# One stream of the expert table for tiles 2 to 4 in place of three tiles of gathers

## The reference

```python
eidx = jnp.take_along_axis(cidx, pos, axis=-1)          # cidx = i1 * 128 + i2
gate = jax.nn.softmax(top, axis=-1)
act = jax.nn.gelu(jnp.einsum('thkd,td->thk', u[eidx], xc), approximate=False)
return jnp.einsum('thk,thkd->td', gate * act, v[eidx])  # u, v: 16384 rows of 1024 floats
```

## Time and profile before

| what | value |
|---|---|
| runs | 4024.05, 4027.4, 4028.98 us |
| the profiled execution | span 4023.9 us; it has no other time of its own, and the runs lie 0.1 to 5.1 us above it |
| first dot product | at 920.8 us |
| last dot product | at 3953.9 us |
| moved by DMA | 1422.97 MB, 1086.75 of it by POOL's queue q0 (the gathers) |
| busy | PE 69%, DVE 61%, POOL 53%, ACT 21% |

### The profile page before, as it was taken

The page is one execution under the profiler, slowest core; times in us unless marked ns, Lnnn a source line. Parts: engine busy times, 40 slices in busy tenths (PEclk is TensorE's granted clock), DMA queues, the critical chain, the costliest instruction groups (busy, mean ns, idle before and its releaser), DMA issues.

```text
span 4023.9 us, 41489 instructions
## 1 busy us (share of the span) xinstructions
PE 2788.8 (69%) x14155; PEld 1429.4 (36%) x14155; DVE 2439.3 (61%) x5186; ACT 858.2 (21%) x2057; POOL 2121.6 (53%) x2149
## 2 busy tenths in 40 slices
PE   6899999898975677796676767455757753333334
PEld 4787777544342322333333323122323320000000
DVE  4552446527676666556766665677766667666652
ACT  4333213402143301112333011132320110000000
POOL 1000205013576656556766565676665667777775
PEclk9999999999987888897887888778888875565566
DMA  8944865567999999999999999999999999999998
GB/s 223 258 154 143 228 209 169 180 240 268 413 407 393 403 410 412 413 412 393 393 400 405 412 400 413 401 406 397 392 406 411 389 409 409 410 408 408 402 409 336
DMA packets 472416, 1422.97 MB, mean 354 GB/s; under 512 B 66152, under 2 KB 136784, under 8 KB 464016
## 3 DMA queue, kind: packets, MB, share of 16 engines
q0 software_dynamic: 298768, 1086.75, 69.5%
q1 hardware_dynamic: 173152, 332.95, 23.2%
q10 hardware_dynamic: 288, 0.62, 0.1%
HBM read 1359.46 MB, written 90.06 MB: 360 GB/s over the span
## 4 chain that ended last, share of the span: by engine, by line
DMA 38%; POOL 13%; PE 9%; issue 8%; DVE 8%; ACT 0%; SPq 0%; DVEq 0%; ACTq 0%; POOLq 0%
DMA ring<-in_peer_u,idx 34%; POOL ring L2459 6%; POOL ring L2452 6%; PE ps_l L1775 5%; DMA ring<-in_peer_v,idxT 4%; DVE ring L2637 4%; PE acc L2683 2%; PE ps_l L1853 1%; PE ps_l L1831 0%; DMA lane<-state_scr 0%; DVE e_f L2560 0%; PE ps_l L1848 0%; DVE hit L2558 0%; DVE where L2520 0%; DVE rest L2521 0%
## 5 line engine op out<-in xcount | busy, mean ns | idle before, releaser
L2637 DVE CUSTOM_DVE_ANT_0 ring<-ring,ps_n2F 128x1024 f32<-128x1024 f32 x1024 | 1242.2, 1220 | 933.3 <-DMA ring<-in_peer_u,idx 922.2
L2459 POOL DMA_INDIRECT ring<-in_peer_u,idx x1024 | 999.1, 976 | 805.8 <-DVE dots L2637 576.3
L2683 PE MATMUL acc<-ring,spread 128*32 128x512 f32 x4096 | 734.7, 853 | 953.3 <-DMA ring<-in_peer_v,idxT 953.1
L2452 POOL DMA_INDIRECT ring<-in_peer_v,idxT x1024 | 993.0, 970 | 336.5 <-issue 297.5
L1775 PE MATMUL ps_l<-lane 128*128 128x512 f32 x1760 | 790.2, 603 | 11.6 <-ACT lane L2100 6.6
L2683 PEld LDWEIGHTS acc<-ring,spread 128*32 128x32 f32 x4096 | 147.7, 136 | 1417.6 <-issue 1415.7
L1775 PEld LDWEIGHTS ps_l<-lane 128*128 128x128 f32 x1760 | 330.8, 193 | 443.8 <-issue 431.4
L562 POOL DMA_DIRECT2D bias<-rpb_scr x16 | 13.2, 829 | 322.5 <-PE ps_dt L846 277.0
L1970 PE MATMUL ps_l<-lane 128*128 128x512 f32 x192 | 117.3, 696 | 56.1 <-DVE nmax L2152 55.8
L2489 ACT ACTIVATE dots<-dots 128x32 f32<-128x32 f32 x32 | 7.3, 229 | 606.1 <-DVE dots L2637 605.9
L2060 ACT ACTIVATE st<-st,nmax 128x512 f32<-128x512 f32 x128 | 92.2, 720 | 184.0 <-DVE nmax L2152 182.9
(11 more groups left out here) (363 smaller groups left out, 4014.7 us busy)
## 6 DMA issues: line engine op xcount, KB each, us to landing
lane<-kept_scr SPq DMA_DIRECT2D x44, 2048.0 KB, 10.6
w_z<-in_w_in SPq DMA_DIRECT2D x16, 1024.0 KB, 6.0
adaB<-in_w_ada SPq DMA_DIRECT2D x16, 1024.0 KB, 6.2
ring<-in_peer_u,idx POOLq DMA_INDIRECT x1024
ring<-in_peer_v,idxT POOLq DMA_INDIRECT x1024, 13.8
kept_scr<-in_w_in SPq DMA_DIRECT2D x6, 2048.0 KB
lane<-w_scr SPq DMA_DIRECT2D x6, 2048.0 KB, 10.9
ada<-in_w_ada SPq DMA_DIRECT2D x8, 1024.0 KB, 15.4
```

Source lines behind the costliest of these rows:

```text
L2452: pool.indirect_dma_start(v_rows[:, nv % RV, :], None, a["peer_v"][0], bass.IndirectOffsetOnAxis(ap=idxT[:, m % 2, col:col + 1], axis=0)). ...
L2459: pool.indirect_dma_start(u_rows[:, n % RU, :], None, a["peer_u"][0], bass.IndirectOffsetOnAxis(ap=idx[:, i % RI, j:j + 1], axis=0)).then_ ...
L2637: nc.vector.tensor_tensor_reduce(out=u_rows[:, n % RU, :], in0=u_rows[:, n % RU, :], in1=ps_n[:, :], scale=1.0, scalar=0.0, op0=ALU.mult, ...
L2683: last = nc.tensor.matmul(acc[q * QUAD:(q + 1) * QUAD, cols], spread[:, m % 2, c0:c0 + QUAD], v_rows[:, nv % RV, cols], start=(g == 0 and ...
```

## The change

V of tiles 2, 3 and 4 is no longer gathered. Their picks and weights are kept (`idx_f` and `weight` get RH = 4 rows) until the tile's 128 picks are weighted, then:

1. PE transposes the tile's picks and weights (`turn_picks`), and DVE splits the expert's number into its two keys (`split_picks`).
2. For each token ACT makes a one-hot matrix of the first key (two instructions: the square of the difference, and relu(1 - 2 x), 128 picks x 128 keys), DVE one of the second key times the weight (`second_hot`), and PE multiplies them (`make_parts`): the token's weight for each of the 128 x 128 experts. Four tokens go together; ACT evicts them to a buffer for 16 tokens, and then stores the buffer (1 MB, in pieces of 512 bytes) in the main memory. This goes on in the slots of the tile after, a batch of four tokens every three slots.
3. From slot 770 to 1046 SP loads the table V once, 32 blocks of 2 MB (four first keys each), and the stored weights, 16 x 3 loads of 512 KB; PE multiplies each block (192 units of four matmuls 128x128 by 512, `multiply_block`) and DVE adds each unit's result to a sum in SBUF (`add_block`). The buffers are those of the lane.
4. At the end DVE norms the three tiles together (`whole_sum` and what follows).

V of the other tiles is gathered as before; that of tiles 0 and 1 is spread over the slots of tiles 0 to 4 (a gather every 2.5 slots), that of tiles 5 to 7 keeps its slots. The ring of V is 10 rows, of which 7 are used until slot 768; the residual of a tile has a row of its own.

```diff
-    RU, RV, RI = 6, 12, 2
+    RU, RV, RI, RH = 6, 10, 2, 4
...
+        parts = v_rows[:, RV - 2:RV, :].rearrange("p r d -> p (r d)")
...
-        TURN_I_AT, IDXT_AT = 14, 20
-        FETCH_AT, SUM_AT = 13, 16
+        TURN_I_AT, IDXT_AT, TURN_W_AT, SPREAD_AT = -26, -25, -9, -8
+        FETCH_AT = 45
+        PICK_TURN_AT, SPLIT_AT, PART_AT, PART_STEP = 4, 5, 9, 3
...
+        pace = GRAINS * (DENSE[-1] + 1) / (GRAINS * len(BEFORE))
+
+        def fetch_slot(s, k):
+
+            m = v_grain[s]
+            if m < GRAINS * DENSE[0]:
+                return FETCH_AT + int(pace * (s * GRAIN + k))
+            return m * GRAIN + FETCH_AT + k
+
+        ALL_ROWS_FROM = PICKS * len(BEFORE) + 84
+        v_row = [nv % (RV - 3) if nv < ALL_ROWS_FROM else (nv - ALL_ROWS_FROM) % RV for nv in range(len(SUMMED) * PICKS)]
...
+            n += PART_AT - PICK_TURN_AT
+            for k in range(P // TURNS):
+                while turning & {n, n + 1}:
+                    n += 1
+                part_mm_at[n], part_ev_at[n + 1] = i * P // TURNS + k, i * P // TURNS + k
+                for r, before in enumerate((2, 2, 1, 1)):
+                    hot_at.setdefault(n - before, []).append(i * P + k * TURNS + r)
+                n += PART_STEP
...
+        DENSE_FROM, DENSE_TO, DENSE_LAG = PICKS * 6 + 2, PICKS * TT + 22, 2
+        unit_slot = [DENSE_FROM + q * (DENSE_TO - DENSE_FROM) // ALL_BLOCK_UNITS for q in range(ALL_BLOCK_UNITS)]
...
+        def load_shares(sp, c):
...
+            if c >= 2:
+                sp.wait_ge(block_mm, (c - 1) * UNITS_A_SHARE)
+            sp.dma_start(v_block[:, c % 2, :, :], v_blocks[c]).then_inc(s_block[c % 2], 16)
+            s, first = divmod(c * KEYS_TOGETHER, PART_KEYS)
+            if first == 0:
+                if s == 0:
+                    sp.wait_ge(s_stored, 16 * ND * P // PART_TOKENS)
+                for i in range(ND):
+                    sp.dma_start(shares[s % 2][i], share_scr[i][s].rearrange("b g n -> b (g n)")).then_inc(s_part[s % 2], 16)
...
                 (ScalarE, in its slot)
+                        for u in hot_at.get(n, ()):
+                            act.wait_ge(picks_split, u // P + 1)
+                            if u >= TURNS:
+                                act.wait_ge(part_mm, u - TURNS + 1)
+                            if u:
+                                act.wait_ge(hot_a_done, u)
+                            nc.scalar.activation(off_key, every_key[:, :], ACT.Square, bias=pickT[:, 0, u % P:u % P + 1], scale=1.0).then_inc(squared, 1)
+                            act.wait_ge(squared, u + 1)
+                            nc.scalar.activation(hot_a[:, u % TURNS, :], off_key, ACT.Relu, bias=1.0, scale=-2.0).then_inc(hot_a_done, 1)
+                        if n in part_ev_at:
+                            k = part_ev_at[n]
+                            group, turn = divmod(k * TURNS, PART_TOKENS)
+                            act.wait_ge(part_mm, (k + 1) * TURNS)
+                            if k and turn == 0:
+                                act.wait_ge(s_stored, 16 * group)
+                            nc.scalar.activation(parts.rearrange("p (c t e) -> p t c e", t=PART_TOKENS, e=PART_KEYS)[:, turn:turn + TURNS, :, :],
+                                                 ps_turn[:, :].rearrange("p (t c e) -> p t c e", t=TURNS, e=PART_KEYS), ACT.Copy).then_inc(part_ev, 1)
+                            if turn == PART_TOKENS - TURNS:
+                                act.wait_ge(part_ev, k + 1)
+                                d, g = divmod(group, P // PART_TOKENS)
+                                nc.scalar.dma_start(share_scr[d][:, :, g, :].rearrange("c b n -> b c n"),
+                                                    parts.rearrange("p (c n) -> p c n", n=PART_KEYS * PART_TOKENS)).then_inc(s_stored, 16)
...
                 (VectorE)
+                def second_hot(u):
+
+                    if u >= TURNS:
+                        v.wait_ge(part_mm, u - TURNS + 1)
+                    k = u % P
+                    nc.vector.tensor_scalar(hot_b[:, u % TURNS, :], every_key[:, :], pickT[:, 1, k:k + 1], pickT[:, 2, k:k + 1], ALU.is_equal, ALU.mult).then_inc(hot_b_done, 1)
+
+                def add_block(q):
...
+                    v.wait_ge(block_mm, q + 1)
+                    if c == 0:
+                        nc.vector.tensor_copy(total, bank).then_inc(block_added, 1)
+                    else:
+                        v.wait_ge(block_added, q - UNITS_A_SHARE + 1)
+                        nc.vector.tensor_tensor(total, total, bank, ALU.add).then_inc(block_added, 1)
...
                 (TensorE)
+                def make_parts(k):
+
+                    pe.wait_ge(hot_a_done, (k + 1) * TURNS)
+                    pe.wait_ge(hot_b_done, (k + 1) * TURNS)
+                    turned_bank_read("parts", k)
+                    for r in range(TURNS):
+                        nc.tensor.matmul(ps_turn[:, r * P:(r + 1) * P], hot_b[:, r, :], hot_a[:, r, :], start=True, stop=True).then_inc(part_mm, 1)
+
+                def multiply_block(q):
...
+                    if q % UNITS_A_SHARE == 0:
+                        pe.wait_ge(s_block[c % 2], 16 * (c // 2 + 1))
+                        s = c * KEYS_TOGETHER // PART_KEYS
+                        pe.wait_ge(s_part[s % 2], 16 * ND * (s // 2 + 1))
+                    if q >= LANE_BANKS:
+                        pe.wait_ge(block_added, q - LANE_BANKS + 1)
+                    s, first = divmod(c * KEYS_TOGETHER, PART_KEYS)
+                    share = shares[s % 2][i].rearrange("p (n e) -> p e n", e=PART_KEYS)
+                    for k in range(KEYS_TOGETHER):
+                        last = nc.tensor.matmul(bank, share[:, first + k, :], v_block[:, c % 2, k, half * HALF:(half + 1) * HALF],
+                                                start=(k == 0), stop=(k == KEYS_TOGETHER - 1))
+                    last.then_inc(block_mm, 1)
```

More of the change, by code:

```diff
@@ L2387, in normed_row @@
             return tok[:, [k for k, kind in enumerate(tok_kind) if kind == ("n2", t)][0] % RT, :]
+        SUMMED = [t for t in range(TT) if t not in DENSE]
+        BEFORE = [t for t in SUMMED if t < DENSE[0]]
+        order = {t: i for i, t in enumerate(SUMMED)}
+        v_grain = [GRAINS * t + g for t in SUMMED for g in range(GRAINS)]
+        pace = GRAINS * (DENSE[-1] + 1) / (GRAINS * len(BEFORE))
[4 more added lines that the diff above has]
+            return m * GRAIN + FETCH_AT + k
@@ new lines, in stage_tail @@
+        for c in range(SHARES):
+            block_at.setdefault(unit_slot[(c - 1) * UNITS_A_SHARE] + 1 if c >= 2 else DENSE_FROM - 6 + c, []).append(c)
+        WHOLE_SUM = DENSE_TO + DENSE_LAG + 2
+        RESIDUAL_SLOT, WHOLE_ROOT, WHOLE_NORM = PICKS * (TT - 1) + 8, WHOLE_SUM + 3 * ND + 1, WHOLE_SUM + 3 * ND + 4
+        LANE_JOBS = len(evac_of)
+        LANE_ACTS, LANE_DVES = acts, dves
+        DROOM = KEYS_TOGETHER * DM
+        v_block = lane[:, 0:2 * DROOM].rearrange("p (r a d) -> p r a d", r=2, a=KEYS_TOGETHER)
@@ new lines, in stage_tail @@
+        share_rooms = [lane[:, 2 * DROOM + r * DM:2 * DROOM + (r + 1) * DM] for r in range(2 * ND - 1)] + [gin[:, 0:2, :].rearrange("p r n -> p (r n)")]
+        shares = [[share_rooms[r * ND + i] for i in range(ND)] for r in range(2)]
+        whole = [st_room[:, 0:DM], st_room[:, DM:2 * DM], qcol[:, :, :, :].rearrange("p r k n -> p (r k n)")]
+        residual = [tok[:, 0, :], tok[:, 1, :], n2[:, :]]
+        v_blocks = a["peer_v"][0].rearrange("(c i b) d -> c b i d", i=KEYS_TOGETHER, b=NKEYS)
@@ L2440, in _ @@
                         n = i * PICKS + j
-                        m, k = fetched(n)
-                        if m is not None:
+                        for m, k in fetch_at.get(n, ()):
                             nv = m * GRAIN + k
@@ L2566, in experts @@
                         v.wait_ge(u_used, (t - RI) * PICKS + (g + 1) * GRAIN)
[L2567 removed]
+                    nc.vector.tensor_copy(idx[:, t % RI, picks], idx_f[:, t % RH, picks]).then_inc(topk_done, 1)
                     if t >= 2:
@@ L2645, in _, with turned_bank_read @@
             def _(pe):
+                turned_last = [None]
+                def turned_bank_read(kind, number):
+                    if turned_last[0] is not None:
+                        was, i = turned_last[0]
+                        if was == "index":
+                            pe.wait_ge(idxT_done, i + 1)
+                        elif was == "weight":
+                            pe.wait_ge(spread_done, TOGETHER * (i + 1))
+                        elif was == "picks":
+                            pe.wait_ge(picks_split, i + 1)
+                        else:
+                            pe.wait_ge(part_ev, i + 1)
+                    turned_last[0] = kind, number
                 def turn(src, c0, done):
```

311 lines of the change are left out of this document (221 added, 90 removed).

## The result

The changed kernel takes 4200.4 us, the median of 4 runs (4199.2 to 4207.5), beside 4028.1 of the kernel before: ratio 1.0438 (95% interval 1.0423 to 1.0453), slower by 172 us. The forecast was slower by 24 (4051), with 4180 as its upper end. The profiled execution spans 4197.5 us.

What follows compares the result with a forecast made beforehand. DMA time was taken as the bound; by stretch, -199 (tiles 0 to 2), -44 (3 to 5) and +267 (6, 7 and the end) made +24 on 4023.9 us, so 4051 us, range 3905 to 4180.

Steps and rivals of the forecast that it cites:

- Tiles 0 to 2: First stretch, 1184.3 us before: DMA floor 915 plus 70 us gives 985, a gain of 199 us (bounds 269 and 124).
- 92% and 97% at once were never shown: First three tiles: doubt that DVE (848 us) and PE (885 us) could stay so busy near the 915 us DMA floor.
- rival 1: All tiles: DMA stays full throughout; 174 us less, 3853 us, or 3950 with half the margins; chance 0.31.
- I take 3 us a time: 63: Tiles 3 to 5: DVE's stand when ACT waits for a store's landing, 0 to 11 us possible, 21 times.
- 43 for the tie: Tiles 3 to 5: cost of ACT, DVE and PE waiting on each other through four reused one-hot buffers, 43 us.
- the floor of 1034: Tiles 3 to 5: DMA time from 1184.2 us, 235 less for fewer V gathers, 85 more for the stores.
- The stretch's own worst case: Tiles 3 to 5: loss of 116 us, at 21 x 11 = 231 for store waits and 35 more for the tie.
- rival 2: Tiles 3 to 5: store landing becomes ACT's clock, DVE stands 227 us in place of 63; 4215 us; chance 0.14.
- Tiles 6, 7 and the end: Last stretch, 734.7 us before: 876 DMA, 18 for taking turns, 108 after the last dot product; 1002, loss 267.
- rival 3: Tiles 6 and 7: PE becomes the bound through a lower clock grant; loss 363 in place of 267; 4147 us; chance 0.08.
- The rule on strided weights: Block multiply in tiles 6 and 7: weight columns 32 bytes apart might load dearer; the forecast included no such price.
- rival 4: Tiles 6 and 7: strided weight loads cost four times, 0.745 us, a unit 6.0 us; 4398 us; chance 0.05.

## Why the prediction was wrong, by its steps

*Tiles 0 to 2: right.* 985 forecast, 999.5 measured, at share 0.95. "92% and 97% at once were never shown" was the right doubt, and rival 1 (DMA full throughout) fell here.

*Tiles 3 to 5: the step that failed.* The prediction put it so: "Under a store the gathers still get most of the engines and six rows of U wait landed, so I take 3 us a time: 63", and "With 43 for the tie: 1140". Of the 138 us that were missing, 77 belong to the store, 40 to the one-hots and 20 to the floor of 1034 under both: it measured 1054.0, at a share of 1.00 with neither store wait nor one-hots. (The stretch's own worst case, a loss of 116, was added up with 35 for the tie, less than the forecast's 43; with 35 on top of the 43 it is 159.)

- The store's wait measured 140 us in place of 63, 6.7 us a time in place of 3. Its place was in the text, and its first step too: DVE "can go on about five slots (13.5 us) from the store". In the store shown above, issued at 2218.1, DVE's last dot product starts 12.6 us later. Three things were mis-sized behind this.
  - The landing. The text bounded it by 7.2 and 24.3 us and took a stand of 3 us from the low part of its 0 to 11. The median landing was 18.6, but it is no one number: the 24 stores took 5.8 to 32.6 us, 6 of them less than the lower bound and 8 more than the upper. A mean hides this, since a short landing gives nothing back: with the 21 awaited landings one by one, the text's own rule (landing less 13.5, where it is positive) adds up to 131.
  - The start behind the landing, which the text puts at nothing. In the store shown the rule gives 24.4 - 13.5 = 10.9 us, and DVE stood 18.1, because ACT's evictions and PE's lane matmuls came first.
  - The way. In its sum the text lets DVE stand by its one-hots alone; in the run with few one-hots that way is closed, and the wait costs 141 all the same. So it is partly luck that 131 comes near 140.

  The earlier trace rows had given a sign: eight packets an engine, 1.3 us of its time at the price of the earlier trace rows, needed 6.6 us to land beside full DMA engines. Of two ends, the nearest row is the one taken under the same load; the engines of the earlier trace rows, busy 54.2%, were the wrong neighbour.
- The one-hots measured 83 in place of 43, and most of it not as a tie: eight buffers took 8 us off. The page has these rows for them (xcount | busy us, mean ns | idle before):

```profile
L2757 DVE TENSOR_SCALAR ring<-every_key,ring 128x128 f32<-128x128 f32 x384 | 118.7, 351 | 181.5 <-PE ps_turn L2928 180.4
...
L2612 ACT ACTIVATE ring<-every_key,ring 128x128 f32<-128x128 f32 x384 | 153.7, 400 | 264.1 <-PE ps_turn L2928 142.4
...
L2621 ACT ACTIVATE ring<-ps_turn 128x512 f32<-128x512 f32 x96 | 56.0, 583 | 244.6 <-DMA share_scr_t<-ring 207.6
L2614 ACT ACTIVATE ring<-ring 128x128 f32<-128x128 f32 x384 | 118.8, 309 | 12.1
```

  ACT's 329 us (364 forecast) are below the price; DVE's 118.7 are over the bound of 113, by little. "None of the three passes 1034 alone" was true and did not help: the 95 us on DVE and the 243 on ACT cost 36 and 43 here, though both engines stay below the bound. That a chain through engines that work in order hides only part of such time is the reading of these runs; how much of it is the engines' time and how much the waits between them was not told apart further.

So rival 2 is in the main what happened ("the store's landing becomes ACT's clock", deciding "from a landing of about 13.5 us on"): the 14 waits of ACT were 14.8 us each in the mean, over its sign of 12, and the DMA share of 0.86 just missed its sign of under 0.85. That its 4215 stands so near 4200.4 is luck: it had 227 for the store where 140 measured, and the one-hots (40 over the forecast), the floor (20) and tiles 0 to 2 (15) made up most of the difference. It had a chance of 0.14.

The Trainium skill, "DMA: Bandwidth & Descriptors", section "Queues, rings and completion order", says that an engine takes turns between its queues by packets of about 9 to 17 descriptors. A store has 128 pieces an engine, 8 to 15 such turns; with a gather's eight rows an engine (1.29 us) between and 3.5 us for the pieces this makes 14 to 23 us, an estimate. The median of 18.6 lies within it, but the single landings, 5.8 to 32.6, go beyond it on both sides, and beyond the 24.3 of taking turns with single rows too. So these runs do not tell the two apart, and neither is a bound.

*Tiles 6, 7 and the end: right.* 1002 forecast, 998.6 measured: 886.7 + 111.9 against 894 + 108. PE is 89% busy at a granted clock of 0.94 (rival 3 fell), and DMA at share 1.02 sets the time.

*The rule on strided weights.* The page's rows:

```profile
L2946 PE MATMUL ps_l<-lane 128*128 128x512 f32 x1280 | 584.7, 611 | 5.6 <-DMA lane<-share_scr_t 5.5
...
L1791 PEld LDWEIGHTS ps_l<-lane 128*128 128x128 f32 x1760 | 335.9, 196 | 489.0 <-issue 462.4
L2946 PEld LDWEIGHTS ps_l<-lane 128*128 128x128 f32 x1280 | 396.6, 315 | 200.4 <-issue 62.1
...
L2928 PEld LDWEIGHTS ps_turn<-ring 128*128 128x128 f32 x768 | 123.6, 239 | 228.9 <-ACT ring L2614 141.8
```

A load with a step of 32 bytes takes 315 ns where neighbouring columns take 196 (L1791) to 239 (L2928). The Trainium skill, "SBUF — State Buffer", section "Door 1: The DMA port swizzle", says that each access which crosses to a new 16-byte line pays a penalty, and the trace agrees in kind, with 1.3 to 1.6 times. At 0.315 us it is shorter than a matmul record of 0.46 (584.7 us by 1280), and PE's matmuls of the units stood idle for nothing but 5.6 us, so rival 4 (over 0.4 us a load) fell.

## What to carry to other kernels

Price a wait for a landing by the landing under the load that will be there. Look at its spread, for a wait pays for the long ones and gets nothing back for the short ones, and count the pieces and not the bytes alone: moving the same 1 MB in longer pieces was worth over 110 us of 4200 here, once the loads that then read the short pieces were asked for earlier and by two queues. Ask of each wait how long the engines behind it can go on (here about 13 us), by which other work the stop reaches them, and how long they need to start again. And an engine below the bound isn't free when a chain ties it to two others in order: here 95 us of DVE work, with its waits, cost 36, and 243 us of ACT work 43.

## What the runs showed of the hardware that was not expected

- With 2048 pieces of 512 bytes a store of 1 MB landed in 18.6 us (median of 24; 5.8 to 32.6) beside the gathers; with 8 KB in a stretch, in 8.2 (3.9 to 13.9; the run with pieces loaded early). A load of 512 KB went from 18.0 to 31.3 us when its pieces became 512 bytes.
- DVE's tensor_scalar with two scalars read from SBUF, 128x128, takes 351 ns a record (118.7 us busy for 384), more than the 295 of the one record at 128x256 in the earlier trace rows.
- Weight loads with a step of 32 bytes: 315 ns, against 196 and 239 with neighbouring columns.
